# State-space batch steps moved against the attention blocks, and VectorE's batch work and parameter work in more pieces

## The reference

```python
def s5_mixer(u, a_re, a_im, log_dt, b_re, b_im, c_re, c_im, d_skip, w_glu, b_glu):
    dt = jnp.exp(log_dt)[:, None]
    a_bar = jnp.exp(dt * a)                        # a = a_re + i a_im, (groups, states)
    b_bar = ((a_bar - 1.0) / a)[..., None] * b
    bu = jnp.einsum('bsgc,gpc->bsgp', uf, b_bar)
    _, states = lax.associative_scan(combine, (a_bar, bu), axis=1)
    y = jnp.real(jnp.einsum('bsgp,gcp->bsgc', states, c))
    y = gelu(y + d_skip * uf)
    return y * sigmoid(y @ w_glu + b_glu)
```

## Time and profile before

| | |
|---|---|
| runs | 3254.61 us median of 3 (3253.44 to 3259.25) |
| profiled execution | 3254.53 us, span of the records 3252.7 us |
| TensorE busy | 3089.1 us, 95% of the span |
| VectorE busy | 1380.0 us, 42% |
| ScalarE busy | 868.3 us, 27% |
| GpSimd busy | 408.2 us, 13% |
| mean granted TensorE clock | 0.976 of full speed |
| chain that ended last | TensorE 90%, VectorE 5%, ScalarE 2%, issue 2% |
| attention and state-space batches | about 2095 to 2345 us |

### The profile page before, as it was taken

How to read it: one execution, slowest core, us unless ns; L and a number is a source line. 1 busy time by engine, 2 the same in 40 slices (tenths; PEclk the granted TensorE clock), 3 DMA queues, 4 the chain that set the end, 5 groups by cost and what they waited for, 6 DMA issues and landing times.

```text
span 3252.7 us, 36883 instructions
## 1 busy us (share of the span) xinstructions
PE 3089.1 (95%) x14144; PEld 2546.1 (78%) x14144; DVE 1380.0 (42%) x1783; ACT 868.3 (27%) x1316; POOL 408.2 (13%) x1012
## 2 busy tenths in 40 slices
PE   7999999999998989999999989988888999999997
PEld 5777888888887777888888878877767888888885
DVE  5654444444445443333333363244435233333335
ACT  5523222211123342111121241144434211121112
POOL 0000000000000004888800000011101000000001
PEclk9999999999999999999999999989989999999998
DMA  3121111111111121232211221111113111111113
GB/s 121 39 78 65 59 52 52 45 39 45 52 52 39 52 72 48 90 109 83 88 45 64 97 85 65 70 66 48 38 65 117 59 46 40 51 58 45 39 52 117
DMA packets 54410, 206.99 MB, mean 64 GB/s; under 512 B 7216, under 2 KB 7984, under 8 KB 52000
## 3 DMA queue, kind: packets, MB, share of 16 engines
q1 hardware_dynamic: 37440, 136.33, 12.1%
q0 software_dynamic: 16864, 69.22, 5.8%
HBM read 173.15 MB, written 31.20 MB: 63 GB/s over the span
## 4 chain that ended last, share of the span: by engine, by line
PE 90%; DVE 5%; ACT 2%; issue 2%; DMA 0%; SPq 0%; POOL 0%; DVEq 0%; ACTq 0%
PE ps L126 28%; PE ps L128 27%; PE ps L127 27%; PE ps L1652 2%; PE ps L262 1%; PE ps L1616 1%; PE ps L1642 1%; DVE acc L815 1%; DVE region_b L121 1%; PE ps L1422 1%; DVE acc L177 1%; DVE acc L185 1%; PE ps L1417 0%; ACT region_b L117 0%; PE ps L1429 0%
## 5 line engine op out<-in xcount | busy, mean ns | idle before, releaser
L126 PE MATMUL ps<-region_a,region_b 128*128 128x512 f32 x1664 | 659.3, 396 | 19.4 <-DVE region_a L221 9.8
L127 PE MATMUL ps<-region_a,region_b 128*128 128x512 f32 x1664 | 651.7, 392 | 0.0
L128 PE MATMUL ps<-region_a,region_b 128*128 128x512 f32 x1664 | 651.4, 391 | 0.0
L815 DVE TENSOR_TENSOR acc<-acc,ps 128x1024 f32<-128x1024 f32 x288 | 351.1, 1220 | 332.6 <-PE ps L128 332.6
L126 PE MATMUL ps<-region_b,region_a 128*128 128x512 f32 x1088 | 433.3, 398 | 17.3 <-DVE region_b L121 9.9
L127 PE MATMUL ps<-region_b,region_a 128*128 128x512 f32 x1088 | 428.7, 394 | 0.0
L128 PE MATMUL ps<-region_b,region_a 128*128 128x512 f32 x1088 | 428.7, 394 | 0.0
L121 DVE TENSOR_TENSOR region_b<-raw,region_b 128x1024 fp32r<-128x1024 f32 x176 | 216.1, 1243 | 394.8 <-ACT region_b L117 394.4
L126 PEld LDWEIGHTS ps<-region_a,region_b 128*128 128x128 f32 x1664 | 314.9, 189 | 87.6 <-issue 10.0
L128 PEld LDWEIGHTS ps<-region_a,region_b 128*128 128x128 f32 x1664 | 314.7, 189 | 65.9
L127 PEld LDWEIGHTS ps<-region_a,region_b 128*128 128x128 f32 x1664 | 315.0, 189 | 64.8 <-issue 1.7
(11 more groups left out here) (286 smaller groups left out, 3343.9 us busy)
## 6 DMA issues: line engine op xcount, KB each, us to landing
raw<-stream SPq DMA_DIRECT2D x252, 512.0 KB, 3.2
ssm_row<-ssm_mid POOLq DMA_DIRECT2D x8, 1632.0 KB, 7.1
x_mid<-acc POOLq DMA_DIRECT2D x24, 512.0 KB, 3.0
ssm_mid<-made_osc POOLq DMA_DIRECT2D x8, 1024.0 KB, 4.5
ssm_mid<-made_out POOLq DMA_DIRECT2D x8, 608.0 KB, 3.5
acc<-x SPq DMA_DIRECT2D x8, 512.0 KB, 7.9
rold<-x POOLq DMA_DIRECT2D x16, 256.0 KB, 3.6
old_a<-x_mid POOLq DMA_DIRECT2D x8, 512.0 KB, 8.6
```

The costliest lines, as they stand in the source:

```text
L126: nc.tensor.matmul(psum, lhs(0), rhs(0), start=first, stop=False)
L127: nc.tensor.matmul(psum, lhs(0), rhs(1), start=False, stop=False)
L128: return nc.tensor.matmul(psum, lhs(1), rhs(0), start=False, stop=last)
L815: nc.vector.tensor_tensor(acc[:, t, :], acc[:, t, :], src, ALU.add).then_inc(F.sem["de"], 1)
```

## The change

Four things are done. No arithmetic is added or taken away.

1. **Steps shifted.** The kernel product of batch b+1 and ScalarE's copy of it stand at step 5 of batch b (that of batch 0 in the projection ahead of attention, behind the first scores; its copy before the first exponential). The transposes come at steps 0 to 2, the scan products at 3 and 4, the inputs of the next batch at 3. The output product stays at step 7 and waits for the kernel copy of the next batch as well.
2. **VectorE's batch work in four pieces.** `m1b` at step 3 and `m2b` at step 4, ahead of the finishing of the block before; the sum with the four scans at step 5 and the two halves of `ob` at step 6, behind it (`ssm_rest_dve`).
3. **The diagonal.** `ssm_skip_dve` of batch b+1 stands at step 6 of batch b, that of batch 0 at its step 0.
4. **Parameters.** `ssm_factors_dve` is cut into `ssm_growth_dve` (8 instructions), `ssm_inverse_dve` (6) and `ssm_factors_dve` (9), which hang behind copies 1, 3 and 5 of down(0). With `ssm_angle_dve`, which stays, the work is in four pieces.

```diff
-        def feed_on_dve(dve, F, last_hooks, hooks={}):
+        def feed_on_dve(dve, F, last_hooks, hooks={}, first_down={}):
             feed_steps(dve, F, lambda c, par, cp, hk: feed_dve_up(dve, F, c, par, cp, hooks),
-                       lambda c, par: feed_dve_down(dve, F, c), {}, lambda: feed_finish_dve(dve, F, last_hooks))
+                       lambda c, par: feed_dve_down(dve, F, c, first_down if isinstance(c, int) and c == 0 else {}),
+                       {}, lambda: feed_finish_dve(dve, F, last_hooks))
...
                     pe.wait_ge(v_out, NT)
                     scores_pair(pe, 0)
+                    ssm_kernel_pe(pe, 0)
...
-        def ssm_factors_dve(dve):
+        def ssm_growth_dve(dve):
...
+        def ssm_inverse_dve(dve):
+            tt = nc.vector.tensor_tensor
+            link = lambda ins: link_dve(dve, ins)
             link(tt(x1, e1, UR, ALU.mult))
             link(tt(x1, x1, cm1, ALU.add))
...
+        def ssm_factors_dve(dve):
+            ts, tt = nc.vector.tensor_scalar, nc.vector.tensor_tensor
+            link = lambda ins: link_dve(dve, ins)
             link(tt(x0, SAI, aim, ALU.mult))
             link(tt(e1, x1, are, ALU.mult))
...
-            dve.wait_ge(buf_in[b % 2], 16 * (b // 2 + 1))
-            dve.wait_ge(s5_s, 2 * b + part + 1)
+            if part < 2:
+                dve.wait_ge(buf_in[b % 2], 16 * (b // 2 + 1))
+                dve.wait_ge(s5_s, 2 * b + part + 1)
             if part == 0:
                 nc.vector.tensor_tensor(v(m1b), bank, cs, ALU.mult).then_inc(s5_m, 1)
-                return
...
+            elif part == 1:
+                nc.vector.scalar_tensor_tensor(out=v(m2b), in0=bank, scalar=nsgn, in1=sn_, op0=ALU.mult,
+                                               op1=ALU.mult).then_inc(s5_m, 1)
+            elif part == 2:
+                dve.wait_ge(s5_m, 2 * b + 2)
+                link(nc.vector.tensor_tensor(m1b[:, :], m1b[:, :], m2b[:, :], ALU.add))
+                for i in range(GB):
+                    g = GB * b + i
+                    ins = nc.vector.tensor_tensor_scan(yb[:, i, :], rho[:, g:g + 1].to_broadcast([P, P]),
+                                                       m1b[:, i * P:(i + 1) * P], 0.0, ALU.mult, ALU.add)
+                link(ins)
+            else:
+                if b == 0:
+                    link(nc.vector.memset(ob[:, :, :, 0:1], 0.0))
+                else:
+                    dve.wait_ge(s5_y, b)
+                nc.vector.scalar_tensor_tensor(out=ob[:, 0, :, 1:], in0=yb[:, :, :], scalar=nsgn, in1=cs,
+                                               op0=ALU.mult, op1=ALU.mult)
+                nc.vector.scalar_tensor_tensor(out=ob[:, 1, :, 1:], in0=yb[:, :, :], scalar=-1.0, in1=sn_,
+                                               op0=ALU.mult, op1=ALU.mult).then_inc(s5_o, 1)
...
-            if s == 0:
-                pe.wait_ge(buf_in[b % 2], 16 * (b // 2 + 1))
-                if b:
-                    pe.wait_ge(s5_g, b)
-                for i in range(GB):
-                    last = nc.tensor.matmul(bank[i][0:GROUP], bf["nbb"][:, i, :], bf["VV"][:, i, 0:P], start=True, stop=True)
-                last.then_inc(kk_done, 1)
-            elif s <= 3:
-                if s == 1:
+            if s <= 2:
+                if s == 0:
                     pe.wait_ge(kk_out, b + 1)
+                    if b:
+                        pe.wait_ge(s5_g, b)
                 else:
-                    pe.wait_ge(s5_cp, 3 * b + s - 1)
-                if s == 3:
+                    pe.wait_ge(s5_cp, 3 * b + s)
+                if s == 2:
                     pe.wait_ge(ub_made, b + 1)
-                src = (bf["Z"], bf["ZS"], ub)[s - 1]
+                src = (bf["Z"], bf["ZS"], ub)[s]
                 for i in range(GB):
                     last = nc.tensor.transpose(bank[i], src[:, i, :], ident[:, :])
                 last.then_inc(s5_tr, 1)
-            elif s <= 5:
-                pe.wait_ge(*((s5_cp, 3 * b + 3) if s == 4 else (s5_m, 2 * b + 1)))
+            elif s <= 4:
+                pe.wait_ge(*((s5_cp, 3 * b + 3) if s == 3 else (s5_m, 2 * b + 1)))
                 for i in range(GB):
-                    last = nc.tensor.matmul(bank[i], zt[:, s - 4, i * P:(i + 1) * P], zt[:, 2, i * P:(i + 1) * P],
+                    last = nc.tensor.matmul(bank[i], zt[:, s - 3, i * P:(i + 1) * P], zt[:, 2, i * P:(i + 1) * P],
                                             start=True, stop=True)
                 last.then_inc(s5_s, 1)
+            elif s == 5 and b + 1 < NB:
+                pe.wait_ge(s5_m, 2 * b + 2)
+                ssm_kernel_pe(pe, b + 1)
             elif s == 7:
                 pe.wait_ge(t_in, 16 * GT * (b + 1))
                 pe.wait_ge(s5_o, b + 1)
+                pe.wait_ge(*((kk_out, b + 2) if b + 1 < NB else (s5_m, 2 * b + 2)))
                 for i in range(GB):
                     nc.tensor.matmul(bank[i], zt[:, 2, i * P:(i + 1) * P], bf["T"][:, i, :], start=True, stop=False)
                     nc.tensor.matmul(bank[i], ob[:, 0, i, 0:P], bf["VV"][:, i, GROUP:9 * GROUP], start=False, stop=False)
...
                                             stop=True)
                 last.then_inc(s5_y, 1)
 
+        def ssm_kernel_pe(pe, b):
+
+            bf = bufs_ssm[b % 2]
+            pe.wait_ge(buf_in[b % 2], 16 * (b // 2 + 1))
+            for i in range(GB):
+                last = nc.tensor.matmul(ps[0:GROUP, 7, i * P:(i + 1) * P], bf["nbb"][:, i, :], bf["VV"][:, i, 0:P],
+                                        start=True, stop=True)
+            last.then_inc(kk_done, 1)
...
...
+            if s <= 2:
+                act.wait_ge(s5_tr, 3 * b + s + 1)
                 if b >= 2:
                     act.wait_ge(s5_y, b - 1)
-                nc.scalar.activation(ztb[:, b % 2, s - 1, :], ps[:, 7, :], ACT.Copy).then_inc(s5_cp, 1)
-            elif s == 4 and b + 1 < NB:
+                nc.scalar.activation(ztb[:, b % 2, s, :], ps[:, 7, :], ACT.Copy).then_inc(s5_cp, 1)
+            elif s == 3 and b + 1 < NB:
                 ssm_inputs_act(act, b + 1)
+            elif s == 5 and b + 1 < NB:
+                ssm_kernel_act(act, b + 1)
             elif s == 7:
                 act.wait_ge(s5_y, b + 1)
                 nc.scalar.activation(group_columns(b), ps[:, 7, :].rearrange("p (g t c) -> p g t c", g=GB, t=GT),
                                      ACT.Copy).then_inc(s5_g, 1)
 
+        def ssm_kernel_act(act, b):
+
+            act.wait_ge(kk_done, b + 1)
+            if b:
+                act.wait_ge(t_in, 16 * GT * b)
+            nc.scalar.activation(kkb[0:GROUP, :, :].rearrange("p a b -> p (a b)"), ps[0:GROUP, 7, :],
+                                 ACT.Copy).then_inc(kk_out, 1)
+
         def ssm_step_dve(dve, n):
             b, s = divmod(n, NT)
-            if s == 2:
-                ssm_skip_dve(dve, b)
-            if s == 5:
-                ssm_scan_dve(dve, b, 0)
-            if s == 6:
-                ssm_scan_dve(dve, b, 1)
+            if 3 <= s <= 4:
+                ssm_scan_dve(dve, b, s - 3)
+
+        def ssm_rest_dve(dve, n):
+            b, s = divmod(n, NT)
+            if 5 <= s <= 6:
+                ssm_scan_dve(dve, b, s - 3)
+            if n == 0:
+                ssm_skip_dve(dve, 0)
+            if s == 6 and b + 1 < NB:
+                ssm_skip_dve(dve, b + 1)
...
             act.wait_ge(u_out, GT)
+            ssm_kernel_act(act, 0)
             ssm_inputs_act(act, 0)
...
                 ssm_step_dve(dve, n)
                 if n:
                     finish(n - 1)
+                ssm_rest_dve(dve, n)
             finish(NA - 1)
...
-            feed_on_dve(dve, ffn1, mix2_norm_hooks(dve), {(1, 1): lambda: ssm_angle_dve(dve),
-                                                          (1, 3): lambda: ssm_factors_dve(dve)})
+            feed_on_dve(dve, ffn1, mix2_norm_hooks(dve), {(1, 1): lambda: ssm_angle_dve(dve)},
+                        {1: lambda: ssm_growth_dve(dve), 3: lambda: ssm_inverse_dve(dve),
+                         5: lambda: ssm_factors_dve(dve)})
```

## The result

| | before | after |
|---|---|---|
| runs, median | 3254.03 us of 4 (3249.81 to 3259.25) | 3210.44 us of 4 (3208.11 to 3213.33) |
| profiled execution | 3254.53 us, span 3252.7 | 3209.60 us, span 3207.4 |
| mean granted clock | 0.976 | 0.983 |

The ratio is 0.9867, with a 95% interval of 0.9851 to 0.9883: 43.6 us faster by the medians, where 34.4 were forecast. The time lies in the range, at its fast end. Two of the 22 runs of the kernel before that were timed beside the experiments took 5902 and 13000 us, in a slower state, and are left out of the ratios.

What follows compares the result with a forecast made beforehand. TensorE, busy 95%, was taken as the bound, so only its standing still and half clock could be won. 7.2 + 8.2 + 16.7 + 4.0 - 1.7 = 34.4 us off 3254.5 gave 3220 us, range 3209 to 3237.

Steps and rivals of the forecast that it cites:

- First down step: Feed-forward: cutting up the parameter work removes TensorE's 4.8 us wait and 2.4 us of half clock; 7.2 us gained.
- GpSimd's later factors: Feed-forward: GpSimd gets its factors some 11 us later, costing nothing because it has 223 us idle after its tables.
- Start of the attention: Batch 0's kernel product moves into the projection, its copy before the first exponential; together 1.7 us lost.
- The waits: Attention: `m1b` waits go in all batches; `ob` waits shrink to 2.4 us (batches 0, 2, 4, 6) and 0.9 (others).
- terms of 2.05 and 2.8 us a batch: Attention: 2.05 us gained in each of batches 0, 2, 4, 6; 2.8 in batch 3, likewise 1 and 5 before clock gain.
- The clock: Attention: half clock regained, 4.0 us of some 8 in batches 0, 2, 4, 6, and 2.9 each in 1 and 5.
- The clock stays up: Rival: TensorE keeps full clock in all attention batches; 4 us more gained, 3216 us; chance 0.15.
- The clock keeps falling: Rival: the clock falls behind each wait for `ob`, in long-block batches too; 15.6 us less gained, 3236 us; chance 0.12.
- The wait for `ob` unshortened: Rival: VectorE's pieces still run one behind the other between waits for TensorE; 3230 us; chance 0.15.
- The parameter pieces: Rival, first down step: the pieces hold up copies as long as the block of 23 did; 3227 us; chance 0.05.
- The transfers: Attention: Toeplitz copies issued directly behind the 1632 KB row load stay hidden, with 2 to 6 us to spare.
- the fifth rival: Toeplitz copies queued behind the row load land after step 5 and hold up ScalarE's exponentials; slower, 3262 us; chance 0.03.

Runs made afterwards that it cites:

- e1: The kernel before with only the parameter work cut into pieces of 8, 6 and 9 instructions; 3247.09 us, ratio 0.9978 to the kernel before.
- e4: The changed kernel with sum, scans and `ob` also ahead of the finish of the block before, still one piece a step; 3202.12 us.
- e3: The changed kernel with VectorE's work from `m2b` to `ob` undivided at step 4, ahead of the finish of block 3; 3234.73 us.
- e2: The changed kernel with the 23 parameter instructions back in one piece ahead of the first down step; 3218.08 us.
- e7: The changed kernel with GpSimd's Toeplitz copies of the next batch issued ahead of the row load, not behind it; 3211.35 us.

## Why the forecast held, and where it was off

**First down step: right.** 7.2 us were forecast by taking the wait and its half clock away. The step is 21.76 us where it was 29.0, with no wait, and e1 alone gives 7.2 (3.9 to 10.4). That GpSimd's later factors cost nothing agrees with the sum.

**Start of the attention: right.** 1.7 us were to be lost, 1.5 were.

**The waits: right in sum, in part by luck.** By the terms of 2.05 and 2.8 us a batch, the attention was to be 19.1 us shorter without any clock gain (8.2 + 16.7 less 2 x 2.9). The waits in it fell by 19.3. That the two are so close is luck: in a short batch the waits fell by 2.6 us (1.32 and 3.20 before, 0.19 and 1.75 after), not by 2.05, and in batches 1 and 5 by 1.8 and not 2.8, since there had been no wait for `ob` in them before. Singly: the wait for `m1b` went in all batches as forecast, the one for `m2b` is 0.19 (forecast 0.2), the one for `ob` in long batches 0.87 to 1.00 (0.9). In short batches it is 1.74 to 1.90 and not 2.4, so 10.8 us in all and not the 13 forecast. The chain on VectorE was too long in my sum: from the start of the sum to the output product it takes 4.71 us (2157.52 to 2162.23), I had 5.1: mainly the maximum, its readout and the finish of block 5 lie closer together (2159.64 to 2160.78, 1.14 us) than the 1.45 of my single durations. And TensorE's own work ends 2.96 us after that start, I had 2.6.

**The clock: the mis-sized term.** I counted 4.0 us in the short batches and 2 x 2.9 in batches 1 and 5, together 9.8. 18.9 were regained, 17.5 of them outside waits, where they shorten the run: 7.7 of the 9.2 us by which the forecast missed. Windows of the kernel before, around five of its seven half-clock stretches (the other two, in batches 4 and 6, read 0.66 and 0.83 over 10 us like those of batches 2 and 0):

```profile
2098.00:2108.00 10.00, 9.58 (x46) 6.75 (x46) 3.31 (x17) 5.63 (x16) 3.81 (x8) 0.66 0.57 224
2116.00:2126.00 10.00, 6.66 (x42) 5.97 (x40) 4.71 (x13) 2.16 (x6) 0.56 (x1) 0.83 0.10 21
2146.00:2160.00 14.00, 14.00 (x83) 13.66 (x83) 5.30 (x16) 2.44 (x5) 0.00 (x0) 0.63 0.00 1
2180.00:2190.00 10.00, 7.44 (x38) 6.94 (x40) 3.83 (x12) 1.40 (x3) 0.56 (x1) 0.66 0.09 18
...
2269.00:2283.00 14.00, 11.69 (x66) 11.35 (x67) 7.59 (x21) 4.01 (x7) 0.00 (x0) 0.63 0.00 1
```

Length times (1 - clock) gives 5.2 us in each of batches 1 and 5, not the 2.9 by which they are longer than batch 3: batch 3 has a wait of 1.34 us for `ob` that batches 1 and 5 don't have, since the slow matmuls covered it, so the comparison of lengths hid a part of the loss. The short batches lose 1.7, 3.4, 3.4 and 1.7, together 10.2. The forecast has about 8, though four times its own 2.5 for batch 2 is 10; and of these it took half. Regained are 10.4 in the long ones and 8.5 in the short ones, where one stretch of 1.7 stays: it fell behind one wait of four, not behind two.

**Which rival was near.** "The clock stays up" gave 3216 and is the nearest; it is true in all batches but one. "The clock keeps falling", which went with the Trainium skill's rule on small idle spells (TensorE: Matmul & The Clock Gate, A second HAM failure mode: psum-queue depth-cycling), did not come: the changed kernel keeps full clock through seven of its eight waits for `ob` and all four for `m2b`. The wait for `ob` unshortened did not come, but its mechanism is there in part: the sum stands behind a finish that waits 0.95 us for TensorE, and e4, where it doesn't, has 1.3 us less of that wait. What e3 shows is the reverse, a finish behind batch work that TensorE waits for. The parameter pieces hold nothing up. The transfers did what the fifth rival needs as its first step (6.5 us to landing, not 1.8), and are done by about 2142.66 + 0.56 + 4.07 + 6.5, so 2154 us (GpSimd's load is issued at 2142.66, the copies behind it in 4.07 us), ahead of ScalarE's kernel copy at step 5:

```profile
2143.22 4.07 POOL L1406 DMA_DIRECT2D toep<-kkb  x8
...
2156.43 0.59 ACT L1488 ACTIVATE kkb<-ps 16x512 f32<-16x512 f32 x1 [0.75 <-PE ps L1452]
```

ScalarE waits only for TensorE there. That small copies land later behind a load is what the forecast took from the rule on rings (the Trainium skill, DMA: Bandwidth & Descriptors, Queues, rings and completion order), and the 6.5 us against 1.8 agree with it. The copies stay hidden, as forecast.

## What to carry to other kernels

Where an engine's wait brings its clock down, price the wait and the slow stretch behind it as two terms, and read the second from windows of granted clock: a comparison of lengths hides what the slow work covers. Split the late engine's work so that what the bound engine waits for next (here the finish of a block) never stands behind more than one piece: in e3, behind 4 us of it, that cost 24 us. And don't put a piece behind an instruction that itself waits for the bound engine (here the same finish): e4, which differs from the change in only that, is about 8 us better. And a single stretch in which a wait did no harm says little, since the same wait can go either way.

## What the runs showed of the hardware

- The granted clock behind a wait of TensorE between matmul groups, over the batches of all nine kernels: behind waits of 1.50 us and less I found none in which it fell. With 1.74 to 1.90 us it fell 3 times of 12, each time in batch 4; these are three kernels with the same waits (the changed one, e2 and e7), so hardly three findings. With 2.40 to 2.86 us it fell 9 times of 10 (the one that didn't is batch 3 of the kernel before), with 2.95 to 3.34 us 16 times of 16. The wait ahead of the first transposes of the attention, 2.71 or 3.19 us, isn't counted here; it brought the clock down in all nine. With the longer waits the fall came in several cases before the wait was over. Why batch 4 and not the others at 1.75 us is open.
- A half-clock stretch cost 1.7, 3.4 or 5.2 us here, and the longer waits did not regularly bring the dearer ones.
- The Toeplitz copies, issued by GpSimd right behind a load of 1632 KB in the same queue, land late: the largest, of 32 KB, after 6.5 us and not 1.8. The load is held a little too, 7.6 us and not 7.0.
